# Experts' weights split in quarters, another order of the DMAs on GpSimd, and moved tiles in a one-layer generator kernel

## What is computed

```
h      = rms_norm(x, g) * (1 + scale) + shift            # 1024 tokens
group  = top1(softmax(h @ w_grp + b_grp))
experts, p = top2(softmax(logits of the 4 experts in the group))
# assignments sorted by expert, each expert's rows padded to blocks of 128
for block (xb, e) in blocks:                              # 31 blocks at most
    gate, up = split(xb @ w_up[e])                        # 1024 -> 2 x 512
    y_rows   = (silu(gate) * up) @ w_down[e]              # 512 -> 1024
x = x + gate2 * sum of y_rows * weight, by token
out = rms_norm(x, g_final)
```

## Time and profile before

| | us |
|---|---|
| median of 3 runs | 2309.19 (2303.57 to 2309.56) |
| the profiled execution | 2308.33 |
| its span, first to last instruction | 2305.9 |
| TensorE busy (matmuls) | 2090.0, 91% |
| VectorE busy | 1462.5, 63% |
| ScalarE busy | 1023.5, 44% |
| GpSimd busy | 824.1, 36% |
| low parts of the experts' weights on VectorE, 186 of 128x2048 | 415.9, mean 2284 ns |
| high parts on ScalarE, 182 of 128x2048 | 337.6, mean 1910 ns |

### The profile page before, as it was taken

How to read it: one execution, slowest core, us unless ns; L and a number is a source line. 1 busy time by engine, 2 the same in 40 slices (tenths; PEclk the granted TensorE clock), 3 DMA queues, 4 the chain that set the end, 5 groups by cost and what they waited for, 6 DMA issues and landing times. The chain is left out here.

```text
span 2305.9 us, 26396 instructions
## 1 busy us (share of the span) xinstructions
PE 2090.0 (91%) x10016; PEld 1727.8 (75%) x10016; DVE 1462.5 (63%) x1711; ACT 1023.5 (44%) x1353; POOL 824.1 (36%) x621
## 2 busy tenths in 40 slices
PE   5899989997999977999999799999599999999992
PEld 3788877775878866888888577787577788877881
DVE  4595543412333327889888355535688999998993
ACT  5323111101444445556655244423266666765763
POOL 8100000002556554667766312200223344434431
PEclk8899999998999987999999899999799999999996
DMA  7334275645556654444554775643589855569425
GB/s 242 80 96 116 55 242 180 209 137 196 170 163 177 180 153 152 140 130 137 143 138 110 224 234 165 214 155 105 219 314 373 282 171 180 159 190 346 103 46 173
DMA packets 269212, 403.40 MB, mean 175 GB/s; under 512 B 31728, under 2 KB 191600, under 8 KB 262304
## 3 DMA queue, kind: packets, MB, share of 16 engines
q1 hardware_dynamic: 240224, 249.57, 34.8%
q0 software_dynamic: 27968, 147.89, 20.5%
q10 hardware_dynamic: 896, 4.28, 0.5%
HBM read 406.37 MB, written 88.67 MB: 215 GB/s over the span
## 5 line engine op out<-in xcount | busy, mean ns | idle before, releaser
L3020 DVE TENSOR_TENSOR ex_w_lo<-ex_raw,ex_w_hi 128x2048 fp32r<-128x2048 f32 x186 | 415.9, 2284 | 42.7 <-ACT ex_w_hi L2882 42.7
L2882 ACT ACTIVATE ex_w_hi<-ex_raw 128x2048 fp32r<-128x2048 f32 x182 | 337.6, 1910 | 178.6 <-DMA ex_raw<-in_w_up_dram,rt_w_rows 80.0
L933 POOL DMA_DIRECT2D vals<-rows_out x40 | 21.8, 545 | 439.5 <-ACT rows_out L925 439.5
L2752 POOL DMA_INDIRECT ex_raw<-in_w_up_dram,rt_w_rows x60 | 74.1, 1235 | 146.9 <-DVE ex_w_lo L3020 141.7
L2752 POOL DMA_INDIRECT ex_raw<-in_w_down_dram,rt_w_rows x30 | 51.9, 1731 | 187.3 <-DVE ex_w_lo L3020 173.9
L925 ACT ACTIVATE rows_out<-rows_ps 128x512 f32<-128x512 f32 x40 | 23.9, 598 | 206.7 <-PE rows_ps L859 206.7
L2494 PE MATMUL mo_ps<-mo_branch_hi,mo_w_hi 128*128 128x512 f32 x256 | 106.3, 415 | 8.2 <-POOL mo_branch_lo L2285 4.2
L1020 PE MATMUL gl_u_ps<-half_hi,gl_u_w_hi 128*128 128x512 f32 x256 | 108.1, 422 | 3.3 <-ACT gl_u_exp L1038 3.3
L1020 PE MATMUL ml_u_ps<-half_hi,ml_u_w_hi 128*128 128x512 f32 x256 | 105.4, 412 | 6.2 <-ACT ml_u_exp L1038 6.2
L2811 PE MATMUL ex_g_ps<-ex_w_hi,ex_x_hi 128*128 128x512 f32 x248 | 103.2, 416 | 6.7 <-DVE ex_x_lo L3025 6.6
L2811 PE MATMUL ex_y_ps<-ex_w_hi,ex_hidden_hi 128*128 128x512 f32 x248 | 100.3, 404 | 7.1 <-DVE ex_w_lo L3020 7.1
(11 more groups left out here) (463 smaller groups left out, 6026.2 us busy)
## 6 DMA issues: line engine op xcount, KB each, us to landing
rows_mod_w<-in_w_mod_dram SPq DMA_DIRECT2D x64, 256.0 KB, 3.5
ml_u_w<-in_w_in_dram SPq DMA_DIRECT2D x32, 512.0 KB, 5.2
gl_u_w<-in_w_in_dram SPq DMA_DIRECT2D x32, 512.0 KB, 5.3
vals<-rows_out POOLq DMA_DIRECT2D x40, 256.0 KB, 3.0
first_values<-vals SPq DMA_DIRECT2D x20, 512.0 KB, 4.2
gl_v<-vals SPq DMA_DIRECT2D x20, 512.0 KB, 3.5
fr_w<-in_w_mod_dram SPq DMA_DIRECT2D x16, 512.0 KB, 12.3
ml_rows<-scan_rows SPq DMA_DIRECT2D x16, 512.0 KB, 5.8
```

Source lines behind the costliest of these rows:

```text
L2752: pool.indirect_dma_start(out=raw[:, q, :], out_offset=None, in_=sources[q], in_offset=bass.IndirectOffsetOnAxis(ap=w_rows[:, q, b:b + 1], ...
L2882: act.activation(hi[:, q, h], raw[:, q, h], ACT.Copy).then_inc(hi_done[q], 1)
L3020: dve.tensor_tensor(lo[:, q, at], raw[:, q, at], hi[:, q, at].bitcast(F32), ALU.subtract)\
```

## The change

It does five things:

1. Weights are split in four quarters of 128x1024 instead of two halves of 128x2048, on ScalarE and VectorE; all waits on these semaphores count four a piece.
2. GpSimd's order in a block is: first up piece, gather, second up piece, add, down piece.
3. Routing on VectorE: the table for the gathers is made first, and the low part of the first piece comes next. Then come the blocks' experts, and the row numbers of each piece apart, with a semaphore for each that `load` waits for. The rows for the adds come last.
4. The triangular mask of the routing's prefix sum moves from the opening into `experts` (`rt_earlier`), which frees 512 bytes a partition for the whole run.
5. Tiles have other addresses: `ex_x` and the other tiles of a block now lie in front of the `rt_` tiles; `c_col` moves to a longer-lived group; three unused tiles of 64 bytes are placed. The mLSTM stage's large tiles and the projections' token tiles start at a multiple of 64 bytes, where before it was 32 over; `ml_c` the reverse. All other tiles keep their place within 64 bytes.

```diff
@@ build_masks @@
-    step(pool.affine_select(out=m.before[:, :], in_=m.ones[:, :], compare_op=ALU.is_gt, fill=0.0,
-                            base=0, pattern=[[1, P]], channel_multiplier=-1))
@@ experts @@
-        HALF = PIECE // 2
+        CUTS = 4
+        CUT = PIECE // CUTS
...
@@ experts, gpsimd @@
+            pool.affine_select(out=earlier[:, :], in_=m.ones[:, :], compare_op=ALU.is_gt, fill=0.0,
+                               base=0, pattern=[[1, P]], channel_multiplier=-1).then_inc(earlier_ready, 1)
...
             def load(b, q):
-                pool.wait_ge(lo_done[q], 2 * b)
+                pool.wait_ge(lo_done[q], CUTS * b)
+                pool.wait_ge(rows_ready[q], 1)
...
                     load(b + 1, 0)
+                if b + 2 < BLOCKS:
+                    gather(b + 2)
+                if b + 1 < BLOCKS:
                     load(b + 1, 1)
+                if b >= 2:
+                    add(b - 2)
                 if b:
                     load(b, 2)
-                if b + 2 < BLOCKS:
-                    gather(b + 2)
-                if b >= 2:
-                    add(b - 2)
@@ experts, tensor @@
-            pe.matmul(cum_ps, m.before[:, :], total, start=True, stop=True)
+            pe.wait_ge(earlier_ready, 1)
+            pe.matmul(cum_ps, earlier[:, :], total, start=True, stop=True)
...
-                    pe.wait_ge(lo_done[q], 2 * b + 2)
+                    pe.wait_ge(lo_done[q], CUTS * (b + 1))
@@ experts, scalar: split_hi @@
-                for h in (slice(0, HALF), slice(HALF, PIECE)):
-                    act.activation(hi[:, q, h], raw[:, q, h], ACT.Copy).then_inc(hi_done[q], 1)
+                for h in range(CUTS):
+                    at = slice(h * CUT, (h + 1) * CUT)
+                    act.activation(hi[:, q, at], raw[:, q, at], ACT.Copy).then_inc(hi_done[q], 1)
@@ experts, vector: find_experts, weight_rows and scatter_rows hold what stood here inline @@
+            def weight_rows(q):
...
+                ts(w_rows[:, q, :], row0[:, :], part[:, q:q + 1], None, ALU.add).then_inc(rows_ready[q], 1)
+                dve.wait_ge(rows_ready[q], 1)
...
             def split_lo(b, q):
-                for h in range(2):
-                    at = slice(h * HALF, (h + 1) * HALF)
-                    dve.wait_ge(hi_done[q], 2 * b + 1 + h)
+                for h in range(CUTS):
+                    at = slice(h * CUT, (h + 1) * CUT)
+                    dve.wait_ge(hi_done[q], CUTS * b + 1 + h)
                     dve.tensor_tensor(lo[:, q, at], raw[:, q, at], hi[:, q, at].bitcast(F32), ALU.subtract)\
                         .then_inc(lo_done[q], 1)
...
             split_lo(0, 0)
+            find_experts()
+            weight_rows(0)
             x_lo(0)
             split_lo(0, 1)
+            weight_rows(1)
+            weight_rows(2)
+            scatter_rows()
@@ the scans: cmat and end_b get a tile behind them @@
+        sb("ml_after_c", [P, 16])
...
+        sb("gl_after_end_b", [P, 16])
@@ build @@
-        m.before = place(top, "before", [P, P])
...
+                m.c_col = place(mls, "c_col", [P, KD])
+                place(mls, "after_c_col", [P, 16])
...
-                    m.c_col = place(split, "c_col", [P, KD])
```

59 lines of the change are left out of this document (32 added, 27 removed).

## The result

The changed kernel takes **2277.12 us** (median of 3 runs, 2276.37 to 2280.82), against 2309.19 before: ratio 0.9873, 95% interval 0.9856 to 0.9891. The profiled execution took 2276.37 us, its span is 2274.7.

The account below looks back on a forecast made before the run. It took late-landing weight pieces as the bound: a full DMA queue until 1830 us, then GpSimd's late queue. From 2308.33 us, -14.3 + 3.0 - 3.5 - 2.5 + 0.2 = -17.1 gave 2291.2 us, range 2280 to 2302.

Parts of the forecast that it names:

- term 1: GpSimd's order after the DMA-bound stretch: block 11's first load issued 3.0 us earlier, no longer behind gather and add.
- term 3: Quarters where VectorE does not wait: six more subtractions per block, pace 17.88 us, +3.0 us over 23 periods.
- the last five blocks: Block 25 to block 30, where nothing is waited for: forecast +0.7 us from the quarters' price.
- the tail: Block 30 to the end: the last down piece, four quarters behind the last results, +0.2 us.
- term 5: Blocks 2 to 9, DMA queue full: order changes nothing, at most 0.4 us a period, seven times, -2.5 us.
- The first rival: Blocks 2 to 9: loads interleave with gather and add, 14.7 us gained instead of 2.5, total 2279.0; chance 0.12.
- Term 6: The rest: last down piece +0.2 us, mask's move 0, new addresses 0 with 3 us allowed to either side.
- agree within 2 us: Expected sign: stages before 1640 us, ahead of the experts' routing, last as long as before within 2 us.
- Terms 1 and 2: Blocks after 9: earlier loads and quarters' shorter waits together remove 14.3 of 15.8 us, leaving 1.5 for two new experts.
- Term 4: Routing to block 0: first gather comes earlier and VectorE's first low part starts 0.9 us earlier, together -3.5 us.
- The low parts' wait: Expected sign: VectorE's wait for ScalarE's high parts falls from 42.7 to 12 to 20 us, all before 1830 us.
- The rival of a fixed 0.16 us more per instruction: Quarters' extra cost unhidden: VectorE's pace 18.39 us, 14.7 us in place of 3.0, total 2302.9; chance 0.06.

Follow-up runs that it names:

- the two parts alone: Kernel before with only the new GpSimd order, 2289.94 us, and kernel before with only quarters in place of halves, 2300.71 us.
- the second profile: The changed kernel measured once more, nothing altered: ratio 0.9883 to the kernel before.
- one padding: Kernel before with only the new tile addresses and the mask's move, less the 64 bytes behind ml_c: 2299.19 us, ratio 0.9978.

## Why the prediction was wrong

Right in mechanism and near in size: the load that waited behind down load, gather and add (term 1), the quarters' steady price (term 3, pace 17.87 against 17.88), the last five blocks (+0.6 against +0.7) and the tail.

- **The step that failed is term 5**, "Order changes nothing in a full queue ... The DMA share of 0.98 leaves at most 0.4 us a period". It was -13.3 us, not -2.5, 10.8 of the 14.8 us by which the sum missed the profiled time (2291.2 against 2276.37); -11.4 in the mean of four kernels on either side. The earlier trace rows had the answer in them: 272 GB/s at a share of 0.94 beside 420 at 1.00. I weighed the share against the throughput, and called the share the bound; the runs show 371 to 395 GB/s at one and the same share. The time under 320 GB/s fell from 35 to 18 us. The first rival said it (126 us for the stretch, 126.7 measured) and had 0.12. That its number was met is in part luck: it named the interleaving alone, and the order alone gave 131.0; the two parts alone gave 9.0 and 5.8 us. Why the quarters take part is open.
- **Term 6, the addresses**: "0, since no wait depends on them and every shape stays". A TensorE-bound stage needs no wait to become shorter. The mLSTM stage gained 3.6 us in the mean. Of the other 3 us of the 6.8 ahead of the routing most are mix_out's spread (336.8 us at a mean clock of 0.971 before, 334.3 at 0.979 after), against "agree within 2 us"; that is luck, and the second profile had none of it.
- **Terms 1 and 2** were -14.3 and measured, in block 9 to 25 with the quarters' price, -10.3 against -12.2. The 1.9 us are in two blocks that fetch new experts, 18.99 and 20.13 us long instead of 17.87, 3.4 above the pace where I had left 1.5. That the two terms would add was wrong too: the order alone was worth 13.8 us there, the quarters on top of it nothing.
- **Term 4** was forecast at -3.5, including 0.9 us for block 0's first low part, and came to 2.3 - 0.5 = 1.8. The gather's issue took 1.80 us beside a subtraction, 0.7 more than the 1.09 of the earlier trace rows, where I had given back 0.5; and with halves and the new order the routing took 30.5 us, so the quarters' share in it was 1.0 and that of the order alone 1.3. With the old order quarters give nothing there (31.8, 32.0).
- The low parts' wait was to be 12 to 20 us and is 7.8, the same miss seen from VectorE.
- The rival of a fixed 0.16 us more per instruction is refuted by the 0.603 us of a 128x512 subtraction. The Trainium skill, VectorE: DVE Perf Modes, "The TRN2 errata", gives their durations well: by its (N+151)/0.96 ns 691, 1224 and 4424 ns for 512, 1024 and 4096 elements (the last two are estimates from its rule), against means of 684, 1219 and 4420 in the profiles. But from start to start, 0.603, 1.135 and 2.20 us for 512, 1024 and 2048 elements, an instruction adds only about 0.07 us to its elements, and the pace is 17.87 us, not the rival's 18.39.

## What to carry to other kernels

A DMA share of 1.00 doesn't say that the transfers are at their limit: put GB/s beside it, stretch by stretch, and if they differ at one share, ask which transfers stand next to which. An edit that shortens a wait by smaller pieces costs instructions wherever nothing waits, so cut only the piece that is waited for, and only as far as the next engine's pace allows. When tiles move, compare the durations of the matmuls before and after, stage by stage: one that TensorE bounds changes its length without any wait. And before a few microseconds of a TensorE-bound stage are given to an edit, compare its granted clock.

## What the runs showed of the hardware that I had not expected

- The same 128x512 matmuls of the mLSTM stage took 397 ns in the median with their stationary operand at 96 modulo 128 bytes, 392 to 394 at 64 and 389 at 0; those of the GLA stage 394 at 64 and 397 at 0; those of the experts 389 and 398 with theirs at 128 and 0 modulo 256. What the rule is was not found, and the places of the stages' other tiles moved too, except between one padding and both, where ml_h and the ml_u tiles alone did.
- Executions of one stage whose matmuls were the same differed by up to 9.5 us, 332.9 to 342.4, with a mean granted clock from 0.98 to 0.95 in it.
- The DMA engines moved 353 to 395 GB/s over six blocks at shares of 0.98 to 1.02.
- In the changed kernel a weight load's issue on GpSimd took 0.99 to 1.03 us where no low-part subtraction, or less than 0.2 us of one, ran beside it (60 of 90), and up to 2.07 us beside one. A gather's took 0.97 us in the one place clear of them, and 1.80 us beside the first low parts, as in these rows of the routing:

```profile
1655.15 4.62 DVE L3040 TENSOR_TENSOR ex_w_lo<-ex_raw,ex_w_hi 128x1024 fp32r<-128x1024 f32 x4
```
```profile
1655.53 1.80 POOL L2767 DMA_INDIRECT ex_x<-moe_in,rt_table  x1 [18.39 <-DVE rt_table L3034]
1657.63 1.86 POOL L2767 DMA_INDIRECT ex_x<-moe_in,rt_table  x1 [0.30 <-issue]
```
